# Softmax attention: ScalarE copies turned weights ahead of the next exponential, and TensorE's step goes transposes, value products, scores

## The chip, the cores and the metric

The kernel runs on one core of a Trainium2 chip. The metric is device time in microseconds (us) of one execution; three runs were taken, and their median counts. Five engines of the core matter here: TensorE (PE in the profile; PEld is its loading of stationary operands), ScalarE (ACT), VectorE (DVE), GpSimd (POOL) and the DMA queues, which SyncE (SP) issues.

## The reference, cut to what matters

The program is two transformer blocks of two layers each, on 256 tokens of width 1024 (the second block has 256 context tokens as well), all in float32. Attention with a softmax occurs in three forms, and only these are touched by the change:

```
# first block, both layers: forgetting attention, 8 heads of 64
logits = where(k_pos <= q_pos, q k^T / 8 + decay, -inf)
# second block, both layers: grouped attention and neighbourhood attention, 8 heads of 64
s = q k^T / 8 (+ bias)          # keys: the latent tokens and the context tokens
p = softmax(logits)
y = p v
```

Stick-breaking attention in the first block and the matrix LSTM in the second run through the same functions of the kernel under other mode names ("stick", "mlstm").

## The kernel before, in words

**The stream of products.** Every dense product is made from float32 weights that arrive by DMA in units of 128 x 1024. ScalarE copies a unit to `w_hi` (line 1055, rounded), VectorE makes the remainder `w_lo` (line 1572), and TensorE makes three products, high by high, high by low and low by high (lines 2438 and 2451 in the mode where 128 tokens are the stationary operand). `w_hi` and `w_lo` have three places (`HL`). A unit is done in parts of 128 tokens: with 256 tokens it has two parts, with 512 tokens four. One part is four matmuls of 512 columns with `w_hi` and two with `w_lo`.

**Steps beside the stream.** Attention is cut into steps, and `spread` and `paced_steps` pin each step to a unit and a part of the stream; after that part TensorE runs the step, in program order. ScalarE and VectorE do their share of the steps of unit j - 2 behind their split of unit j (`stream`, `finish_unit`). Each engine has one queue in program order, so a wait in it holds back all that stands behind it. In the dense part of every attention there is one step to a part of the stream, and a new unit begins before an even step. The grouped and the neighbourhood attention have a first stretch too, where the first four steps lie one to a unit.

**Items.** An item is one head with one tile of 128 queries; items come in pairs of two heads. Item k has 128 or 256 keys in the first block, and in the second 512 keys for latent queries and 256 for context queries (layer 0 only). In layer 0 of the second block two pairs of 256 keys and two pairs of 512 keys alternate; in layer 1 all have 512. There are 64 softmax pairs: 8 in each first-block layer, 16 for each of the two attentions in layer 0 of the second block, 8 for each in layer 1.

**What an item goes through.** (1) TensorE: `pair_scores` writes the scores of items k and k + 1 (line 2751; line 2757 adds a bias or a mask where there is one). (2) VectorE: `begin` takes the negated maximum (line 2111). (3) ScalarE: `weights` makes the exponential with its sum (line 1393) into `prob[k % 2]`, once `turn(k - 2)` has read that place. (4) VectorE: `finish` takes the reciprocal and scales the weights (line 2127). (5) TensorE: `turn` transposes them into PSUM bank 6 (line 2768), once the bank has been copied out. (6) ScalarE: `turned_weights` copies the bank to `prob_t` (line 1413). (7) TensorE: `pair_gather` multiplies with the values (line 2788). (8) ScalarE and VectorE: `output` writes the result of a pair in two parts (lines 1425 and 2160).

**Order in one step k, before.** TensorE: at even k `pair_scores(k)`, then `pair_gather(k - 4)`; at every k `turn(k - 2)`. ScalarE: `weights(k)`, `turned_weights(k - 2)`, `output(k - 3)`. VectorE: `begin(k)`, `finish(k - 1)`, `output(k - 3)`. Items are counted so that `output` does something at even k only.

VectorE's part, which the change leaves as it is:

```
if k < n:
    begin(k)
if 1 <= k <= n:
    finish(k - 1)
if k >= 3:
    output(k - 3)
```

Of the kernel before, what the change touches and what calls it, by code (L numbers as in the profile page):

```python
# [212 lines left out]
def build(nc, a, out):  # L213
    ctx = ExitStack()
    with ctx:
# [806 lines left out]
        def _(act):  # L1022
# [359 lines left out]
            def attend(st, k):  # L1382
                k0 = st.at["item"]
                n = len(st.items)

                def weights(i):
                    e, i0 = st.items[i], k0 + i
                    nk = e["nk"]
                    z = ps[:, 4 + i0 % 2, 0:nk]
                    if st.mode == "soft":  # L1390
                        act.wait_ge(max_done, st.at["max"] + i + 1)
                        act.wait_ge(pt_done, i0 - 1)
                        nc.scalar.activation(prob[:, i0 % 2, 0:nk], z, ACT.Exp, bias=att[:, i0 % 2:i0 % 2 + 1],  # L1393
                                             accum_out=att[:, 2 + i0 % 2:3 + i0 % 2]).then_inc(exp_done, 1)
                    elif st.mode == "stick":
                        act.wait_ge(bounded, st.at["bounded"] + i + 1)
                        act.wait_ge(probs_done, i0 - 1)
                        nc.scalar.activation(st.tmp[:, 2 + i0 % 2, 0:nk], st.tmp[:, i0 % 2, 0:nk], ACT.Sigmoid, scale=-1.0)
                        nc.scalar.activation(st.tmp[:, 4 + i0 % 2, 0:nk], st.tmp[:, i0 % 2, 0:nk], ACT.Sigmoid).then_inc(exp_done, 1)
                    else:  # L1400
                        act.wait_ge(scores_done, i0 + 1)
                        act.wait_ge(probs_done, i0 - 1)
                        for d in range(2):
                            ins = nc.scalar.activation(st.decay[:, i0 % 2, d, 0:nk], ps[:, 4 + d, 0:nk], ACT.Exp,
                                                       bias=st.mcols[:, e["t"], 2 + d, e["h"]:e["h"] + 1])
                        ins.then_inc(exp_done, 1)

                def turned_weights(i):
                    e, i0 = st.items[i], k0 + i
                    bank = 7 if st.mode == "mlstm" else 6  # L1410
                    act.wait_ge(pt_done, i0 + 1)
                    act.wait_ge(pv_done, i0 - 1)
                    nc.scalar.activation(prob_t[:, i0 % 2, 0:e["nk"]], ps[:, bank, 0:e["nk"]], ACT.Copy).then_inc(pt_saved, 1)

                def output(i):
                    e, i0 = st.items[i], k0 + i
                    if st.mode == "mlstm":
                        act.wait_ge(pv_done, i0 + 1)
                        nc.scalar.activation(e["dst"], ps[:, 7, 0:P], ACT.Copy).then_inc(ml_saved, 1)
                    elif e["hh"]:  # L1420
                        pr, t = e["y"]
                        act.wait_ge(pv_done, i0 + 1)
                        if i == 1 and st.y_free:
                            act.wait_ge(main.units_used, st.y_free)
                        nc.scalar.activation(st.ys[0][:, pr, t * P:(t + 1) * P], ps[:, 7, 0:P], ACT.Copy).then_inc(y_hi_done, 1)

                if st.mode == "mlstm":
                    i = k // 2
                    if k % 2 == 0 and i >= 3:
                        output(i - 3)  # L1430
                    if k % 2 and i < n:
                        weights(i)
                    if k % 2 and 2 <= i <= n + 1:
                        turned_weights(i - 2)
                    return
                if k < n:
                    weights(k)
                if 2 <= k <= n + 1:
                    turned_weights(k - 2)
                if k >= 3:  # L1440
                    output(k - 3)
# [896 lines left out]
        def _(pe):  # L2338
# [385 lines left out]
            def attend(st, k):  # L2724
                k0 = st.at["item"]
                n = len(st.items)

                def scores(i):
                    e, i0 = st.items[i], k0 + i
                    nk = e["nk"]  # L2730
                    if st.mode == "mlstm":
                        pe.wait_ge(probs_done, i0)
                        pe.wait_ge(exp_done, i0)
                        for d in range(2):
                            dst = ps[:, 4 + d, :]
                            row = row_of_r[:, e["h"], :]
                            mm(dst[:, 0:nk], row, ml_both[:, d, e["k0"]:e["k0"] + nk], start=True, stop=False)
                            mm(dst[:, 0:T], ident_r[:, :], e["masks"][d], start=False, stop=True)
                        mm(ps[:, 6, 0:nk], e["q"], e["k"], start=True, stop=True).then_inc(scores_done, 1)
                        return  # L2740

                def pair_scores(i):

                    pair = [(st.items[i + hh], ps[:, 4 + (k0 + i + hh) % 2, :]) for hh in range(2)]
                    nk = pair[0][0]["nk"]
                    adds = len(pair[0][0]["add"])
                    n_add = T if adds and nk > T else nk
                    pe.wait_ge(exp_done, k0 + i)
                    for lo, hi in ([(0, nk)] if n_add == nk else [(0, n_add), (n_add, nk)]):
                        for e, z in pair:  # L2750
                            ins = mm(z[:, lo:hi], e["q"], e["k"][:, lo:hi], start=lo == 0, stop=not adds)  # L2751
                    for j in range(adds):
                        for e, z in pair:
                            lhs, rhs, ready = e["add"][j]
                            if ready is not None:
                                pe.wait_ge(bias_ready, ready)
                            ins = mm(z[:, 0:n_add], lhs, rhs, start=False, stop=j == adds - 1)  # L2757
                    ins.then_inc(scores_done, 2)

                def turn(i):  # L2760
                    e, i0 = st.items[i], k0 + i
                    bank = 7 if st.mode == "mlstm" else 6
                    pe.wait_ge(probs_done, i0 + 1)
                    pe.wait_ge(pt_saved, i0)
                    if st.mode == "mlstm":
                        pe.wait_ge(ml_saved, st.at["ml"] + i)
                    for c in range(e["nk"] // P):
                        ins = nc.tensor.transpose(ps[:, bank, c * P:(c + 1) * P], prob[:, i0 % 2, c * P:(c + 1) * P],  # L2768
                                                  ident[:, :])
                    ins.then_inc(pt_done, 1)  # L2770

                def gather(i):
                    e, i0 = st.items[i], k0 + i
                    chunks = e["nk"] // P
                    pe.wait_ge(pt_saved, i0 + 1)
                    for c in range(chunks):
                        ins = mm(ps[:, 7, 0:P], prob_t[:, i0 % 2, c * P:(c + 1) * P], e["v"][c],
                                 start=c == 0, stop=c == chunks - 1)
                    ins.then_inc(pv_done, 1)

                def pair_gather(i):

                    chunks = st.items[i]["nk"] // P
                    pe.wait_ge(pt_saved, k0 + i + 2)
                    pe.wait_ge(y_saved, st.at["pair"] + i // 2)
                    for c in range(chunks):
                        for hh in range(2):
                            ins = mm(ps[hh * HD:(hh + 1) * HD, 7, 0:P], st.items[i + hh]["v"][c],  # L2788
                                     prob_t[:, (k0 + i + hh) % 2, c * P:(c + 1) * P], start=c == 0, stop=c == chunks - 1)
                    ins.then_inc(pv_done, 2)  # L2790

                if st.mode == "mlstm":
                    i = k // 2
                    if k % 2 == 0 and i >= 3:
                        gather(i - 3)
                    if k % 2 and i < n:
                        scores(i)
                    if k % 2 and 2 <= i <= n + 1:
                        turn(i - 2)
                    return  # L2800
                if k % 2 == 0 and k < n:
                    pair_scores(k)
                if k % 2 == 0 and k >= 4:
# [104 lines left out]
```

## Time and profile before

| what | value |
|---|---|
| median of 3 runs | 2824.49 us (2823.5 to 2825.09) |
| profiled execution, its own time | 2821.74 us |
| its span in the profile | 2819.9 us |
| granted TensorE clock, mean | 0.983 of full speed |
| TensorE matmul busy | 2671.0 us (95%) |
| VectorE busy | 1677.2 us (59%) |
| ScalarE busy | 1375.5 us (49%) |
| GpSimd busy | 93.4 us (3%) |
| DMA | 444.88 MB, 158 GB/s in the mean |

Times in the profile are counted from the span's start. A row of the timeline gives the start, the duration, the engine and line, what is written from what, the number of instructions merged into the row, and in brackets how long the engine was idle before and what ended the idle time. The softmax attentions lie at about 130 to 190 and 580 to 640 us (forgetting), 1445 to 1555 and 2425 to 2490 us (grouped), 1560 to 1675 and 2494 to 2570 us (neighbourhood).

### The profile page before, as it was taken

What the parts mean: (1) busy time and instruction counts of PE and PEld (TensorE: products, weight loads), DVE (VectorE), ACT (ScalarE), POOL (GpSimd) and SP (SyncE); (2) the same over time, 40 slices, a digit from 0 to 9 for tenths busy, and PEclk for the clock granted to TensorE, in tenths of its full rate; (3) what the DMA queues carried; (4) which work ended last, traced back from release to release, by engine and by line L of the source; (5) the groups of instructions that cost most, each with busy time, mean ns of one, the idle gap of its engine ahead of it and who ended that gap; (6) DMA issues with size and microseconds to landing.
All of it is one profiled execution on the core that took longest, in us unless ns stands there. A gap on an engine that the chain in (4) does not pass through costs nothing.

```text
span 2819.9 us, 40663 instructions
## 1 busy us (share of the span) xinstructions
PE 2671.0 (95%) x14804; PEld 2147.3 (76%) x14804; DVE 1677.2 (59%) x2555; ACT 1375.5 (49%) x2245; POOL 93.4 (3%) x104
## 2 busy tenths in 40 slices
PE   8999999998999999999999999999998899999998
PEld 7668888666888888777776777777777677667997
DVE  5654445646998998354545545553454556455776
ACT  5544345544777776433335344432333544445654
POOL 2000001000000000000000100000000110010000
PEclk9999999999999999899999999999999999999999
DMA  7438895434999997222221213454552234334564
GB/s 227 130 117 263 252 299 161 127 112 165 312 332 323 321 331 264 84 68 60 83 85 50 78 57 105 129 163 134 150 160 73 83 111 114 89 105 119 144 187 142
DMA packets 352459, 444.88 MB, mean 158 GB/s; under 512 B 19616, under 2 KB 197920, under 8 KB 352288
## 3 DMA queue, kind: packets, MB, share of 16 engines
q1 hardware_dynamic: 349792, 435.44, 49.0%
q0 software_dynamic: 2208, 6.79, 0.8%
q8 instruction: 109, 1.79, 0.3%
q14 instruction: 62, 0.51, 0.1%
q10 hardware_dynamic: 288, 0.36, 0.0%
HBM read 441.48 MB, written 1.05 MB: 157 GB/s over the span
## 4 chain that ended last, share of the span: by engine, by line
PE 79%; DVE 8%; ACT 7%; issue 5%; DMA 1%; POOL 0%; ACTq 0%; DVEq 0%; POOLq 0%
PE ps L2410 20%; PE ps L2438 15%; PE ps L2397 14%; PE ps L2451 7%; PE ps L2442 4%; ACT w_hi L1055 2%; PE ps L2647 2%; PE ps L2768 2%; PE ps L2459 2%; PE ps L2751 2%; PE ps L2757 1%; DVE w_lo L1572 1%; PE ps L2788 1%; PE ps L2475 1%; PE ps L2354 1%
## 5 line engine op out<-in xcount | busy, mean ns | idle before, releaser
L1572 DVE TENSOR_TENSOR w_lo<-raw,w_hi 128x1024 fp32r<-128x1024 f32 (+1 forms) x578 | 683.7, 1199 | 511.2 <-ACT w_hi L1055 447.7
L1055 ACT ACTIVATE w_hi<-raw 128x1024 fp32r<-128x1024 f32 (+1 forms) x578 | 585.6, 1030 | 250.1 <-PE ps L2410 120.6
L2438 PE MATMUL ps<-w_hi,h_hi 128*128 128x512 f32 (+1 forms) x992 | 403.7, 409 | 11.5 <-DVE h_lo L2023 4.0
L2438 PE MATMUL ps<-w_hi,h_lo 128*128 128x512 f32 (+1 forms) x992 | 380.2, 385 | 0.0
L2397 PE MATMUL ps<-h_hi,w_hi 128*128 128x256 f32 (+1 forms) x1008 | 300.5, 323 | 16.4 <-ACT w_hi L1055 11.3
L2451 PE MATMUL ps<-w_lo,h_hi 128*128 128x512 f32 (+1 forms) x992 | 298.1, 384 | 0.0
L2397 PE MATMUL ps<-h_lo,w_hi 128*128 128x256 f32 (+1 forms) x1008 | 295.7, 319 | 0.0
L2397 PEld LDWEIGHTS ps<-h_hi,w_hi 128*128 128x128 f32 x1008 | 191.6, 190 | 49.2 <-ACT w_hi L1055 15.3
L2438 PEld LDWEIGHTS ps<-w_hi,h_hi 128*128 128x128 f32 x992 | 188.2, 190 | 48.5 <-issue 12.7
L2451 PEld LDWEIGHTS ps<-w_lo,h_hi 128*128 128x128 f32 x992 | 183.3, 188 | 39.7
L2438 PEld LDWEIGHTS ps<-w_hi,h_lo 128*128 128x128 f32 x992 | 187.9, 189 | 29.0 <-issue 1.0
L2410 PE MATMUL ps<-w_hi,act_hi 128*128 128x512 f32 x528 | 208.2, 394 | 0.0
L1572 DVE TENSOR_TENSOR w_lo<-arena,w_hi 128x1024 fp32r<-128x1024 f32 (+1 forms) x192 | 201.7, 1086 | 7.5 <-ACT w_hi L1055 7.1
L2410 PE MATMUL ps<-w_hi,act_lo 128*128 128x512 f32 x528 | 205.8, 390 | 0.0
L2397 PEld LDWEIGHTS ps<-h_lo,w_hi 128*128 128x128 f32 x1008 | 191.8, 190 | 12.6
L1393 ACT ACTIVATE arena<-ps,att 128x512 f32<-128x512 f32 (+2 forms) x128 | 72.9, 570 | 244.0 <-DVE att L2111 150.6
L1055 ACT ACTIVATE w_hi<-arena 128x1024 fp32r<-128x1024 f32 (+1 forms) x192 | 175.3, 948 | 23.5 <-PE ps L2410 22.8
L2397 PE MATMUL ps<-h_hi,w_lo 128*128 128x256 f32 (+1 forms) x1008 | 177.2, 318 | 0.0
L2397 PEld LDWEIGHTS ps<-h_hi,w_lo 128*128 128x128 f32 x1008 | 149.8, 191 | 13.1
L2410 PE MATMUL ps<-w_lo,act_hi 128*128 128x512 f32 x528 | 149.6, 394 | 0.6
L2410 PE MATMUL ps<-w_hi,h_hi 128*128 128x512 f32 (+1 forms) x384 | 145.7, 379 | 1.6 <-issue 1.4
L2410 PE MATMUL ps<-w_hi,h_lo 128*128 128x512 f32 (+1 forms) x384 | 142.9, 372 | 0.0
(302 smaller groups left out, 4227.5 us busy)
## 6 DMA issues: line engine op xcount, KB each, us to landing
raw<-in_w_in SPq DMA_DIRECT2D x196, 512.0 KB, 3.7
arena<-in_w_mod SPq DMA_DIRECT2D x96, 512.0 KB, 6.0
raw<-in_w_up SPq DMA_DIRECT2D x88, 512.0 KB, 4.4
raw<-in_w_gu_exp SPq DMA_DIRECT2D x64, 512.0 KB, 5.5
arena<-in_w_gu_exp SPq DMA_DIRECT2D x64, 512.0 KB, 5.0
arena<-in_w_gu_exp SPq DMA_DIRECT2D x64, 384.0 KB, 3.9
arena<-in_w_dn_exp SPq DMA_DIRECT2D x48, 512.0 KB, 6.4
raw<-in_w_gu_dense SPq DMA_DIRECT2D x44, 512.0 KB, 8.1
```

Source lines behind the costliest of these rows:

```text
L1055: nc.scalar.activation(w_hi[:, half, 0:n], place[:, 0:n], ACT.Copy).then_inc(seg.sig.hi_ready, 1)
L1393: nc.scalar.activation(prob[:, i0 % 2, 0:nk], z, ACT.Exp, bias=att[:, i0 % 2:i0 % 2 + 1], accum_out=att[:, 2 + i0 % 2:3 + i0 % 2]).then_in ...
L1572: nc.vector.tensor_tensor(w_lo[:, half, 0:n], place[:, 0:n], w_hi[:, half, 0:n].bitcast(F32), ALU.subtract).then_inc(seg.sig.lo_ready, 1)
L2397: ins = mm(dst, w[:, f0:f0 + wide], x[:, k + c, 0:seg.N], start=upper and k + c == 0 and x is ah, stop=not upper and k + c == DC - 1)
L2410: ins = mm(dst, x, w[:, c * width:(c + 1) * width], start=upper and opens and c == 0 and x is xh, stop=not upper and closes and c == m - 1)
L2438: ins = mm(ps[:, 2 * h + p % 2, 0:width], x[:, k + c, p * P:(p + 1) * P], wh[:, c * width:(c + 1) * width], start=opens and c == 0 and x i ...
L2442: ins = mm(ps[0:wide, 2 * h + p % 2, 0:seg.N], wh[:, f0:f0 + wide], x[:, k + c, 0:seg.N], start=opens and c == 0 and x is ah, stop=False)
L2451: ins = mm(ps[:, 2 * h + p % 2, 0:width], ah[:, k + c, p * P:(p + 1) * P], wl[:, c * width:(c + 1) * width], start=False, stop=last and no ...
L2459: ins = mm(ps[0:wide, 2 * h + p % 2, 0:seg.N], wl[:, f0:f0 + wide], ah[:, k + c, 0:seg.N], start=False, stop=last)
L2647: ins = mm(ps[0:wide, bank, cols_], w[:, f0:f0 + wide], x[:, k + c, cols_], start=begins and kind == 0, stop=ends and kind == 2)
L2751: ins = mm(z[:, lo:hi], e["q"], e["k"][:, lo:hi], start=lo == 0, stop=not adds)
L2768: ins = nc.tensor.transpose(ps[:, bank, c * P:(c + 1) * P], prob[:, i0 % 2, c * P:(c + 1) * P], ident[:, :])
```

## The change

In mode "soft" alone, ScalarE's step becomes `turned_weights(k - 2)`, `weights(k)`, `output(k - 3)`, and TensorE's even step becomes `turn(k - 2)`, `pair_gather(k - 4)`, `pair_scores(k)`; an odd step is `turn(k - 2)` as before. VectorE's order stays. No instruction is added or removed, and no wait is written differently; the modes "stick" and "mlstm" keep their order.

```
@@ attend, ScalarE
+                if st.mode == "soft" and 2 <= k <= n + 1:
+                    turned_weights(k - 2)
                 if k < n:
                     weights(k)
-                if 2 <= k <= n + 1:
+                if st.mode != "soft" and 2 <= k <= n + 1:
                     turned_weights(k - 2)
                 if k >= 3:
                     output(k - 3)
@@ attend, TensorE
+                if st.mode == "soft":
+                    if 2 <= k <= n + 1:
+                        turn(k - 2)
+                    if k % 2 == 0 and k >= 4:
+                        pair_gather(k - 4)
+                    if k % 2 == 0 and k < n:
+                        pair_scores(k)
+                    return
                 if k % 2 == 0 and k < n:
                     pair_scores(k)
                 if k % 2 == 0 and k >= 4:
                     pair_gather(k - 4)
```

## Rows read from the trace of the kernel before

**Rows 1.** The page: busy time, share of the span and instructions of each engine.
```profile
PE 2671.0 (95%) x14804; PEld 2147.3 (76%) x14804; DVE 1677.2 (59%) x2555; ACT 1375.5 (49%) x2245; POOL 93.4 (3%) x104
```

**Rows 2.** Line 2768, the transposes of all modes: its idle time, us and times.
```profile
  issue: 31.9, 123
  DVE arena L2127: 15.7, 27
```

**Rows 3.** Timeline of PEld, layer 1, grouped attention: one pair of steps.
```profile
2450.81 0.30 PEld L2751 LDWEIGHTS ps<-arena 64*128 64x128 f32 x4 [0.35 <-ACT arena L1393]
2451.87 0.85 PEld L2788 LDWEIGHTS ps<-arena 128*64 128x64 f32 x16 [0.76 <-ACT arena L1413]
2452.89 0.42 PEld L2768 LDWEIGHTS ps<-ident,arena 128*128 128x128 f32 x4 [0.17 <-issue]
...
2455.33 0.42 PEld L2768 LDWEIGHTS ps<-ident,arena 128*128 128x128 f32 x4 [0.82 <-DVE arena L2127]
...
2457.30 0.30 PEld L2751 LDWEIGHTS ps<-arena 64*128 64x128 f32 x4 [0.36 <-ACT arena L1393]
```

**Rows 4.** Timeline of ACT over the same pair of steps.
```profile
2453.95 0.69 ACT L1393 ACTIVATE arena<-ps,att 128x512 f32<-128x512 f32 x1 [1.89 <-DVE att L2111]
...
2454.63 0.59 ACT L1413 ACTIVATE arena<-ps 128x512 f32<-128x512 f32 x1
2455.11 0.28 ACT L1425 ACTIVATE y_hi<-ps 128x128 fp32r<-128x128 f32 x1
...
2457.50 1.05 ACT L1055 ACTIVATE w_hi<-raw 128x1024 fp32r<-128x1024 f32 x1
```

**Rows 5.** Timeline of DVE over the same pair of steps.
```profile
2452.09 1.23 DVE L1572 TENSOR_TENSOR w_lo<-raw,w_hi 128x1024 fp32r<-128x1024 f32 x1 [1.69 <-ACT w_hi L1055]
2453.23 0.68 DVE L2111 TENSOR_REDUCE att<-ps 128x1 f32<-128x512 f32 x1
...
2455.42 0.29 DVE L2160 TENSOR_TENSOR y_lo<-ps,y_hi 128x128 fp32r<-128x128 f32 x1 [0.91 <-ACT y_hi L1425]
2455.62 0.68 DVE L2111 TENSOR_REDUCE att<-ps 128x1 f32<-128x512 f32 x1
...
2456.41 0.49 DVE L2127 TENSOR_SCALAR arena<-arena,att 128x512 f32<-128x512 f32 x1
```

**Rows 6.** Timeline, layer 0, grouped: scores of 512 keys and an unhindered maximum.
```profile
1475.79 0.30 PEld L2751 LDWEIGHTS ps<-arena 64*128 64x128 f32 x4 [0.44 <-ACT arena L1393]
...
1476.97 0.69 DVE L2111 TENSOR_REDUCE att<-ps 128x1 f32<-128x512 f32 x1 [1.45 <-PE ps L2751]
```

**Rows 7.** Timelines, layer 1, neighbourhood: scores with bias, and their maximum.
```profile
2494.55 0.73 PEld L2751 LDWEIGHTS ps<-arena 64*128 64x128 f32 x8 [0.35 <-issue]
...
2496.79 0.69 DVE L2111 TENSOR_REDUCE att<-ps 128x1 f32<-128x512 f32 x1 [3.35 <-PE ps L2757]
```

**Rows 8.** Timeline of PEld, layer 0, grouped: a step after scores of 256 keys.
```profile
1510.55 0.85 PEld L2788 LDWEIGHTS ps<-arena 128*64 128x64 f32 x16 [0.33 <-issue]
...
1513.06 0.33 PEld L2768 LDWEIGHTS ps<-ident,arena 128*128 128x128 f32 x2
...
1514.97 0.30 PEld L2751 LDWEIGHTS ps<-arena 64*128 64x128 f32 x4 [0.39 <-ACT arena L1393]
```

**Rows 9.** Timeline of PEld: scores of steps 4 and 28, layer 0, grouped.
```profile
1469.72 0.30 PEld L2751 LDWEIGHTS ps<-arena 64*128 64x128 f32 x4 [1.37 <-ACT arena L1393]
...
1537.85 0.30 PEld L2751 LDWEIGHTS ps<-arena 64*128 64x128 f32 x4 [0.36 <-issue]
```

**Rows 10.** The same, layer 0, neighbourhood.
```profile
1584.65 0.73 PEld L2751 LDWEIGHTS ps<-arena 64*128 64x128 f32 x8 [2.32 <-ACT arena L1393]
...
1657.08 0.73 PEld L2751 LDWEIGHTS ps<-arena 64*128 64x128 f32 x8 [0.37 <-issue]
```

**Rows 11.** The same, layer 1, neighbourhood: scores of steps 8 and 14.
```profile
2531.47 0.73 PEld L2751 LDWEIGHTS ps<-arena 64*128 64x128 f32 x8 [0.36 <-ACT arena L1393]
...
2553.25 0.73 PEld L2751 LDWEIGHTS ps<-arena 64*128 64x128 f32 x8 [0.36 <-ACT arena L1393]
```

## The prediction

> **What bounds the kernel now.** I read the page first: TensorE is busy for 95% of the span, VectorE for 59%, ScalarE for 49% [rows 1]. So the program ends earlier only if TensorE's queue is held less in the attention steps, or gets through them in less time. Then the line view of the transposes: in front of line 2768 the loading of operands sat idle for 31.9 us under "issue" and 15.7 us behind VectorE [rows 2], the largest idle time among the softmax attention's TensorE lines. It covers all modes and also holds a gap of 0.17 us in front of each even step's transposes, which is there without any wait.
>
> Then the timeline, one pair of steps in the grouped attention of layer 1 [rows 3]. Step 6 starts at 2450.81 with the scores, 1.06 later come the value products (a gap of 0.76, as the scores still stream), 1.02 later the transposes. The odd step's transposes start at 2455.33, 2.44 after the even ones, with 0.82 us idle before them. Where nothing is waited for, a stretch of the stream behind transposes takes about 1.2: from the odd transposes to the next scores it is 1.97, less 0.42 for the transposes and 0.36 for the gap before the scores. So 2.44 holds 0.8 of waiting. What it waits for: `turn(7 - 2)` needs bank 6, so `turned_weights(6 - 2)`, the copy at 2454.63, behind the exponential at 2453.95 [rows 4], which waited for the maximum at 2453.23, which stood behind a `w_lo` of 1.23 us at 2452.09 [rows 5]. The copy itself could have started two microseconds earlier: it sits behind an exponential with which it has nothing to do.
>
> **The change part by part.** Nothing is added or removed; two orders change. All times below are for items of 512 keys. T is the start of the even step, s the start of its scores.
>
> *ScalarE's copy first.* The copy of item k - 2 then needs only the transposes at T and the value products that follow, so it runs at about T + 1.7, long before the odd transposes. The 0.8 of waiting goes. But exponential k can no longer be held by transposes either; it waits for its maximum alone.
>
> *TensorE's order.* Before, transposes k had from s to the end of the next step's scores and products. Now they are the first thing in step k + 2. The ring that must close in one pair is: scores, maximum k, exponential k, first output part, second output part, maximum k + 1 (VectorE's order is unchanged), scaling k, transposes k. From rows: scores to maximum 1.18 where nothing hinders it [rows 6]; to the exponential 0.72 (maximum at 2453.23, exponential at 2453.95); to the next ScalarE instruction 0.68 [rows 4], which is now the output and no longer the copy (0.48 saved); to VectorE's output 0.31; to maximum k + 1 0.20; to the scaling 0.79; scaling 0.49 [rows 5]; a hop to TensorE of 0.05, as between the other links. Sum 4.42. TensorE's own work from s to the next T is scores 1.06, stream 1.25, transposes 0.42, stream 1.2, or 3.93. So the ring ends last and a new wait of 0.5 arises at T. It is queued in front of value products and scores, and so all the stream waits for it.
>
> From T to s: transposes 0.42, a gap, products 0.85, a gap. What is the gap between transposes and products, and between products and scores? The trace has neither. Behind products, whose matmuls have 128 columns, the gap is 0.17; behind the stream's 512 columns it is 0.36; behind scores 0.33 [rows 8] to 0.76 [rows 3]. In both new places the work in front is 128 columns wide, so I take 0.17 twice; the ends are 0 and 0.36. With 0.17: s = T + 1.61, and the pair takes 4.42 + 1.61 = 6.03 against 6.49 now. The Trainium skill, TensorEngine Tiling (Array Packing), Key Properties, says that changing the tiling mode drains TensorE. Counted by that rule alone, an unbiased pair has three changes of mode before and after, and a biased one four before and three after, so the order itself would save nothing in the first; the rows add that the length of a gap goes with what is being drained.
>
> *VectorE's and ScalarE's splits.* These stand in the queues before an even step. `w_hi` starts at exponential k + 1 plus 1.16 now (2457.50, against a maximum k + 1 at 2455.62 and 0.72 more) [rows 4, 5]; without the copy it is 0.68, so at s + 3.1 (maximum k + 1) + 0.72 + 0.68 = s + 4.5, ending at s + 5.55. `w_lo` follows until s + 6.8, and maximum k + 2 is due at s + 6.03 + 1.18 = s + 7.2. The split that now delays every such maximum by more than a microsecond fits with 0.4 to spare.
>
> *256 keys.* Scores take 0.63 (the products start 0.33 behind 0.30 of loading [rows 8]). The ring is shorter by about 1.2 (each pass over half the columns), near 3.2; TensorE's work from s to the next T is 0.63 + 1.25 + 0.42 or 0.2 + 1.2 = 3.3 to 3.5. No wait.
>
> **The sum.** Layer 1, grouped: six intervals of 6.49 - 6.03, 2.8 us. Layer 0, grouped: now 68.13 from step 4 to step 28, which is three rounds of four pairs, 22.7 each [rows 9]. After: ring 4.42 twice, 3.5 and 3.4 for the short pairs, and from T to s 1.0, 1.2, 1.6, 1.4 (short and long products and transposes), 20.9; three rounds 5.3 us, with the half round behind them some 5.7. Neighbourhood: with the bias the maximum starts 2.24 behind the scores [rows 7], so its ring is 5.48 and the pair 7.09, against 21.78 / 3 = 7.26 in layer 1 [rows 11]: six intervals, 1.0 us. In layer 0, 72.43 / 3 = 24.14 per round [rows 10] against 20.9 + 2 x 1.06 = 23.1: 3.2 us for three rounds and the rest. Forgetting attention has 128 and 256 keys, and masks that lengthen TensorE's part, so no ring; I give each of 16 pairs the narrower gap in front of its scores, 0.36 - 0.17, 3 us in both layers together. The long waits at the start of the attentions, 1.37 and 2.32 before step 4's scores [rows 9, 10], come from a maximum behind the branches' evacuation; then the transposes wait for a scaling of the same moment, so they stay. Together 2.8 + 5.7 + 1.0 + 3.2 + 3 = 15.7 us. The profiled execution took 2821.74 (span 2819.9), 2.75 below the median; the difference applies to the median of 2824.49 alike: 2808.8, say 2809.
>
> **The rivals.**
>
> *A, forecast:* the waits at the odd transposes go, the ring takes part of it back: 10 to 25 us less, 2799 to 2814. Chance 0.64.
>
> *B, the ring doesn't bind:* if some link is shorter than the rows say, only the removal counts. All idle time of rows 2 is 47.6; less 0.17 in 64 even steps (10.9), less the other modes' and some tenths that the matmuls cover, about 21 remains, and with narrower gaps (64 x 0.19 = 12) the gain is 33: 2791. Against it: each link is a row. Chance 0.08.
>
> *C, the gain is eaten by gaps:* if the two new gaps are 0.36 each as behind the stream, every pair is 0.38 longer, 24 us over 64 pairs; 15.7 - 24 gives 2833, and with half of that 2821, near no change. For it: the trace has neither sequence. Against it: 0.17 behind 128 columns. Of this 0.12 for a result within 6 us of no change, 0.04 above.
>
> *D, slower, a split falls into the ring:* if `w_lo` reaches VectorE less than 1.2 before maximum k is due, the maximum is late by up to 1.23, and the ring passes it on to the stream in full. It decides from 0.4 us of lateness of `w_hi` on. In layer 1 every pair has a split (12 pairs), in layer 0 one pair in two (14): 26 x 1.23 = 32 us lost, minus 15.7, gives 2841; at half the lateness 2825. For it: the slack of 0.4 is small, and ScalarE's tanh of a finished gate stands in the same queue. Against it: the order of VectorE's queue, where `w_lo` comes only after scaling k. Chance 0.12, half of it slower by more than 0.2%.
>
> **How the numbers follow.** About 0.2%, 5.6 us, is what a measurement of this kernel can tell from no change. Faster by more: A, B, 0.03 of C's milder forms, 0.75. Within: 0.09 + 0.05 = 0.14. Slower: 0.04 + 0.07 = 0.11. The range leaves out B's far end and the ends of C and D: 2797 to 2825; A alone 2799 to 2814.
>
> **What the profile after would show.** The copy of line 1413 in front of the exponential, no idle time before odd transposes; new idle time of about 0.5, put down to VectorE's line 2127, in front of even transposes of 512-key pairs; 6.03 from even step to even step in layer 1's grouped attention; gaps of 0.17 in front of products and scores. A gap of 0.36 there speaks for C; a `w_lo` directly before a late maximum k for D; no wait at even transposes for B. I would be wrong in the sign if exponential or maximum stood behind something else that is now late, above all transposes k - 1, whose copy now precedes exponential k + 1 by only some hundredths.

## The result, and the profile after

The changed kernel takes 2815.91 us in the median of 18 runs (2809.76 to 2820.32), beside 2825.41 us in 18 runs of the kernel before (2822.54 to 2827.85): a ratio of 0.9968, 95% interval 0.9961 to 0.9975, 9.5 us less. The forecast was 15.7 us less, 2809, in a range of 2797 to 2825; the measured time lies in that range and some 2 us above rival A's own, 2799 to 2814. The profiled execution took 2815.94 us (span 2814.2).

| stretch, first scores to last value products | before | after | forecast gain | gain |
|---|---|---|---|---|
| forgetting, both layers | 58.29 + 59.51 | 59.29 + 58.20 | 3.0 | 0.3 |
| layer 0, grouped | 106.51 | 103.27 | 5.7 | 3.2 |
| layer 0, neighbourhood | 113.54 | 112.22 | 3.2 | 1.3 |
| layer 1, grouped | 63.47 | 60.30 | 2.8 | 3.2 |
| layer 1, neighbourhood | 72.50 | 72.46 | 1.0 | 0.0 |

Times are us, from the timelines of TensorE's loading, one profile of each kernel. The gains add up to 8.1 us. The two profiled spans differ by 5.7 us, since the parts of the program outside these stretches took 2.4 us more in the profile after. How layer 1's gain is split between its two rows is not firm: in the repeated run of the changed kernel (`h1_change_again`) they read 58.80 and 74.00, with the same sum.

The page of the changed kernel, busy time of each engine (answers to [rows 1]): TensorE does the same work.

```profile
PE 2672.0 (95%) x14804; PEld 2149.9 (76%) x14804; DVE 1676.5 (60%) x2555; ACT 1383.7 (49%) x2245; POOL 95.1 (3%) x104
```

The line of the transposes, now line 2770, idle time before it (answers to [rows 2]), first of the changed kernel, then the third line of the same view of the kernel before, which [rows 2] leaves out:

```profile
  DVE arena L2129: 57.1, 86
  issue: 12.0, 50
```

```profile
  ACT arena L1413: 6.4, 15
```

So the idle time in front of the transposes grew from 54.0 to 69.1 us while the kernel got faster. Over the three lines of the attention (transposes, scores and value products in all modes, without the waits for lines that only other modes have) it shrank: in front of the scores the wait for the exponential (40.6 us before) is gone, in front of the value products 34.3 us became 14.7. This view adds the idle time of the loading and that of the matmuls. Taken apart, the loading's fell from 119.3 to 84.9 us, by 34, and the matmuls' own from 23.5 to 17.2, by 6.3; the time fell by 9.5. Idle time of the loading is mostly not idle time of the matmuls.

The pair of steps in layer 1's grouped attention, loading on TensorE in the changed kernel (answers to [rows 3]; 2770 transposes, 2790 products, 2753 scores):

```profile
2453.59 0.42 PEld L2770 LDWEIGHTS ps<-ident,arena 128*128 128x128 f32 x4 [0.29 <-DVE arena L2129]
2454.18 0.85 PEld L2790 LDWEIGHTS ps<-arena 128*64 128x64 f32 x16 [0.17 <-issue]
2455.20 0.30 PEld L2753 LDWEIGHTS ps<-arena 64*128 64x128 f32 x4 [0.17 <-issue]
...
2457.72 0.42 PEld L2770 LDWEIGHTS ps<-ident,arena 128*128 128x128 f32 x4 [0.21 <-DVE arena L2129]
...
2459.62 0.42 PEld L2770 LDWEIGHTS ps<-ident,arena 128*128 128x128 f32 x4 [0.28 <-DVE arena L2129]
```

From even step to even step 6.03 us, as forecast, and the scores start 1.61 behind the even transposes, as forecast. But the matmuls leave no room in it. The same loop in windows (span of time, its length, busy time of each engine), first of the kernel before, then of the changed one:

```profile
2450.81:2457.30 6.49, 6.08 (x41) 4.04 (x40) 3.83 (x8) 3.64 (x9) 0.00 (x0) 1.00 0.29 81
```

```profile
2453.59:2459.62 6.03, 6.03 (x42) 4.07 (x41) 3.92 (x8) 3.86 (x10) 0.00 (x0) 1.00 0.29 90
```

Before, TensorE's matmuls stood still for 0.41 us of each pair; now for none. The row of the matmuls in the kernel before shows where, in front of the odd transposes, and names the copy:

```profile
2455.36 0.63 PE L2768 MATMUL ps<-ident,arena 128*128 128x128 f32 x4 [0.41 <-ACT arena L1413]
```

The loading's row of the same transposes has 0.82 and names VectorE [rows 3]; half of that time the matmuls in flight had covered.

ScalarE and VectorE in the changed kernel (answers to [rows 4, 5]):

```profile
2455.38 0.60 ACT L1413 ACTIVATE arena<-ps 128x512 f32<-128x512 f32 x1 [0.68 <-PE ps L2790]
2457.11 0.69 ACT L1393 ACTIVATE arena<-ps,att 128x512 f32<-128x512 f32 x1 [1.13 <-DVE att L2113]
...
2457.78 0.27 ACT L1425 ACTIVATE y_hi<-ps 128x128 fp32r<-128x128 f32 x1
```

```profile
2454.74 1.23 DVE L1574 TENSOR_TENSOR w_lo<-raw,w_hi 128x1024 fp32r<-128x1024 f32 x1 [1.20 <-ACT w_hi L1055]
2456.38 0.69 DVE L2113 TENSOR_REDUCE att<-ps 128x1 f32<-128x512 f32 x1 [0.42 <-PE ps L2753]
...
2458.08 0.29 DVE L2162 TENSOR_TENSOR y_lo<-ps,y_hi 128x128 fp32r<-128x128 f32 x1 [0.42 <-ACT y_hi L1425]
2458.29 0.68 DVE L2113 TENSOR_REDUCE att<-ps 128x1 f32<-128x512 f32 x1
...
2459.08 0.49 DVE L2129 TENSOR_SCALAR arena<-arena,att 128x512 f32<-128x512 f32 x1
```

The copy stands ahead of the exponential and waits for nobody's maximum. `w_lo` ends 0.42 us before the even maximum can start, so rival D's split is out of the way. The odd maximum follows `y_lo` directly: the ring of the prediction (a closed chain of waits, in which each pair of steps waits for the one before), link by link. From the scores at 2455.20 to the transposes at 2459.62 it takes 4.42.

### The profile page after: what moved, and what is told of

Same layout as the page of the kernel before. It is cut to its first block, busy times and chain, and to the rows that moved or that the text cites. A ratio compares the mean times of both kernels' runs of the same rounds, so it can differ in the third digit from the quotient of the medians.

```text
span 2814.2 us, 40663 instructions
## 1 busy us (share of the span) xinstructions
PE 2672.0 (95%) x14804; PEld 2149.9 (76%) x14804; DVE 1676.5 (60%) x2555; ACT 1383.7 (49%) x2245; POOL 95.1 (3%) x104
## 4 chain that ended last, share of the span: by engine, by line
PE 82%; DVE 8%; ACT 5%; issue 4%; POOL 0%; DVEq 0%; ACTq 0%; POOLq 0%
PE ps L2412 20%; PE ps L2440 17%; PE ps L2399 14%; PE ps L2453 8%; PE ps L2444 4%; PE ps L2753 2%; PE ps L2770 2%; ACT w_hi L1055 2%; PE ps L2649 2%; PE ps L2461 2%; PE ps L2790 2%; PE ps L2759 1%; PE ps L2477 1%; DVE w_lo L1574 1%; PE ps L2356 1%
```

## The experiments

All ratios are against runs of the kernel before on the same chip. "Pair" is the loop in layer 1's grouped attention, 6.49 before and 6.03 after the change.

### Each half of the change alone

`e1_scalar_only`: the edit on ScalarE is made, the one on TensorE isn't. `e2_tensor_only`: the reverse.

> ScalarE's order of the change with TensorE's order of before. Theory (a wait for the copy goes, and what then ends last is a chain through both outputs and the second maximum): the idle time before the odd transposes goes, but the exponential now waits for transposes and for the copy, and the exponential of item k + 1 reaches the next scores late: about 6.05 us from even step to even step in layer 1's grouped attention, nearly the 6.03 of the full change, so about 2816 us in all. Rival (TensorE's order is what gains): no better than before, 2825. Rival (the copy's wait is all there is, and TensorE's new order costs something): about 5.75 from even step to even step and 2805.

> TensorE's order of the change with ScalarE's order of before. Theory: the copy is back between exponential and output, so the ring from scores to transposes is 0.48 longer, 4.90 and with 1.61 up to the scores 6.51 in layer 1's grouped attention (before: 6.49), 7.57 in its neighbourhood attention (before: 7.26); in all 2824 to 2830. Rival (TensorE's order gains by itself, through narrower gaps): 2815 or less.

ScalarE's order alone: 2816.01 us, ratio 0.9964 (0.9952 to 0.9977), as expected and as much as the whole change; the pair takes 6.00, with matmuls in 5.96 of it. TensorE's order alone: 2861.89 us, ratio 1.0131 (1.0116 to 1.0146); the pair takes 7.28, far over what was expected. ScalarE's rows in that kernel, and TensorE's loading of two sets of transposes, show why:

```profile
2491.38 0.59 ACT L1413 ACTIVATE arena<-ps 128x512 f32<-128x512 f32 x1
2491.85 0.28 ACT L1425 ACTIVATE y_hi<-ps 128x128 fp32r<-128x128 f32 x1
2493.09 0.69 ACT L1393 ACTIVATE arena<-ps,att 128x512 f32<-128x512 f32 x1 [0.96 <-DVE att L2111]
...
2493.77 0.58 ACT L1413 ACTIVATE arena<-ps 128x512 f32<-128x512 f32 x1
```

```profile
2492.08 0.42 PEld L2768 LDWEIGHTS ps<-ident,arena 128*128 128x128 f32 x4 [1.00 <-DVE arena L2127]
2494.47 0.42 PEld L2768 LDWEIGHTS ps<-ident,arena 128*128 128x128 f32 x4 [0.78 <-DVE arena L2127]
```

Each set of transposes starts 0.70 behind a copy (2491.38, 2493.77), because that copy frees their bank. The row of the loading names VectorE's scaling, which had ended 0.8 before; the row of the matmuls names the copy:

```profile
2494.50 0.63 PE L2768 MATMUL ps<-ident,arena 128*128 128x128 f32 x4 [0.37 <-ACT arena L1413]
```

The ring from the scores (2488.80) runs over the maximum 1.17, exponential 0.73, copy 0.68, y_hi 0.47, y_lo 0.31, maximum 0.21, exponential 0.72, copy 0.68 and transposes 0.70, 5.67 in all, and 1.61 more lead to the next scores: 7.28. The expectation had missed that the transposes wait for the copy and not only for the scaling.

### VectorE's scaling in front of the maximum

`e3_scale_first` is the changed kernel, `g2_before_scale_first` the kernel before, both with

```
+                if st.mode == "soft" and 1 <= k <= n:
+                    finish(k - 1)
                 if k < n:
                     begin(k)
-                if 1 <= k <= n:
+                if st.mode != "soft" and 1 <= k <= n:
                     finish(k - 1)
```

> The changed kernel with one more order: VectorE's step of a softmax attention is scaling k - 1, maximum k, output. This takes maximum k + 1 (0.79 us) out of the ring that ends in transposes k. Theory (the ring sets the pair): idle time before the transposes of 512-key pairs goes, 5.75 instead of 6.03 from even step to even step in layer 1's grouped attention, 6.5 to 6.8 instead of 7.08 in its neighbourhood attention, some 10 us less than the changed kernel: about 2806. Rival (TensorE's own work sets the pair, and the waits seen only fill its shadow): no difference from the changed kernel, 2816.

It took 2818.26 us, ratio 0.9974 (0.9964 to 0.9985), nothing gained where 2806 was expected. Its VectorE rows:

```profile
2456.32 0.68 DVE L2113 TENSOR_REDUCE att<-ps 128x1 f32<-128x512 f32 x1
2458.79 1.23 DVE L1574 TENSOR_TENSOR w_lo<-raw,w_hi 128x1024 fp32r<-128x1024 f32 x1 [1.79 <-ACT w_hi L1055]
...
2460.12 0.49 DVE L2129 TENSOR_SCALAR arena<-arena,att 128x512 f32<-128x512 f32 x1
2460.53 0.68 DVE L2113 TENSOR_REDUCE att<-ps 128x1 f32<-128x512 f32 x1
2462.22 0.29 DVE L2162 TENSOR_TENSOR y_lo<-ps,y_hi 128x128 fp32r<-128x128 f32 x1 [1.01 <-ACT y_hi L1425]
...
2463.02 0.68 DVE L2113 TENSOR_REDUCE att<-ps 128x1 f32<-128x512 f32 x1
```

From odd maximum to odd maximum it takes 6.70 us (2456.32 to 2463.02), with no link on TensorE: maximum, exponential, `w_hi`, `w_lo`, scaling, even maximum, exponential, `y_hi`, `y_lo`, scaling, odd maximum. The split of the stream is a part of it. So there is a ring of ScalarE and VectorE that the prediction had not looked for. It did not set every pair of this kernel: the even transposes around it lie 6.09 to 7.25 apart. Layer 1's grouped attention took 64.50 us instead of 60.30, its neighbourhood attention 70.82 instead of 72.46. In the kernel before, the same walk through its rows gives: exponential 0.72, copy 0.68, `w_hi` 0.48, `w_lo` 1.08, maximum 1.14, exponential 0.72, copy 0.68, `y_hi` 0.48, `y_lo` 0.31, maximum 0.20, together 6.49, its pair to the hundredth [rows 3 to 5]. That gave a number to test:

> The kernel before, with VectorE's scaling of item k - 1 put in front of maximum k. Theory 1 (a ring of ScalarE and VectorE sets the pair in the kernel before): both scalings come into that ring: maximum k + 1, exponential 0.72, copy 0.68, w_hi 0.48, w_lo 1.08, reciprocal 1.14, scaling 0.19, maximum 0.41, exponential 0.72, copy 0.68, y_hi 0.48, y_lo 0.31, reciprocal 0.20, scaling 0.19, maximum 0.40: the pair in layer 1's grouped attention goes from 6.49 to 7.68, and the kernel to 2845 or more. Rival (the transposes' wait is what costs, and it ends with a scaling): scaling earlier shortens it, the pair goes below 6.49, and the kernel below 2825.

Measured: 2863.93 us, ratio 1.0135 (1.0120 to 1.0151), and the pair (scores to scores):

```profile
2483.59 0.30 PEld L2753 LDWEIGHTS ps<-arena 64*128 64x128 f32 x4 [0.72 <-ACT arena L1393]
...
2491.27 0.30 PEld L2753 LDWEIGHTS ps<-arena 64*128 64x128 f32 x4 [0.82 <-ACT arena L1393]
```

The pair took 7.68, the sum of the links, and 32 pairs of 512 keys by 1.19 more are 38 us of the 40 that the kernel lost. In the kernel before, then, ScalarE and VectorE set the pace of the 512-key pairs, and the wait at the odd transposes was not what set it.

### Scores as the second part of the step

`e4_scores_second` has ScalarE's old order, and TensorE's even step as transposes, scores, value products.

```
                     if 2 <= k <= n + 1:
                         turn(k - 2)
+                    if k % 2 == 0 and k < n:
+                        pair_scores(k)
                     if k % 2 == 0 and k >= 4:
                         pair_gather(k - 4)
-                    if k % 2 == 0 and k < n:
-                        pair_scores(k)
```

> TensorE's even step goes transposes, scores, value products, with ScalarE's order of before. The scores start 1.02 us earlier in the step, so the ring has 1.02 more room, and the copy of line 1413, which is back in it, costs 0.48. Theory: the ring closes before TensorE is through, about 5.75 in layer 1's grouped attention and 2806 in all. Rival (the scores' place doesn't matter, only the copy's): as before or as with TensorE's order alone, 2825.

2837.20 us, ratio 1.0043 (1.0030 to 1.0056), slower than before, where the theory had 2806 and the rival 2825. The steady pair again takes 6.49 (even transposes at 2455.31, 2461.80 and 2468.29), which fits: TensorE's order isn't in that ring. By stretches most of the loss lies in layer 0, 109.15 and 118.67 us against 106.51 and 113.54; the forgetting attentions and layer 1's neighbourhood attention lost 1.8 each. At the starts of the attentions the transposes wait up to 3.84 us for a scaling. It was not taken apart further.

### Opening the ring of the changed kernel

VectorE's `output` of a pair (`y_lo`) moves from the even step into the next odd one, behind the scaling, so the odd maximum no longer stands behind it:

```
-                if k >= 3:
+                if st.mode == "soft":
+                    if k % 2 and 5 <= k <= n + 1:
+                        output(k - 4)
+                    if k == n + 2:
+                        output(n - 1)
+                elif k >= 3:
                     output(k - 3)
```

> The changed kernel, with VectorE's second output part (y_lo) moved one step later, behind scaling k, so that maximum k + 1 no longer stands behind y_lo. That opens the ring which sets the even transposes' wait: scores to transposes would be about 3.7 and no longer 4.42. Theory 1 (TensorE is full: the matmul rows of the changed kernel cover 6.03 of a pair's 6.03 us, and a pair in the scale-first kernel that waited for nothing took 5.95): the pair in layer 1's grouped attention goes from 6.03 to 5.95, and the kernel gains 1 to 3 us, to about 2814. Rival (the prediction's own count, 3.93 of TensorE's work behind the scores and 1.61 in front of them): the pair goes to 5.55, and the kernel gains 0.48 in some 28 pairs, to about 2803.

> The kernel before, with only that move in VectorE's queue. Theory 1: the 6.49 us of a pair are a ring of ScalarE and VectorE alone (maximum k + 1, exponential 0.72, copy 0.68, w_hi 0.48, w_lo 1.08, maximum 1.14, exponential 0.72, copy 0.68, y_hi 0.48, y_lo 0.31, maximum k + 1 0.20: sum 6.49), and the wait at the odd transposes is only what TensorE shows of it. The move takes y_hi, y_lo out of the ring: pair about 6.0, TensorE's own work, and the kernel near 2816, as much as the whole change, with its two edits left out. Rival (the prediction's reading: the copy behind the exponential in front of the odd transposes costs 0.8): that copy stays, so the pair stays at 6.4 to 6.5 and the kernel at 2825.

> ScalarE's new order alone, with that move in VectorE's queue. Theory 1: with ScalarE's order alone a pair takes 6.00, with a wait of 0.48 in front of the scores, but matmuls fill 5.96 of it; the move opens that ring, the wait goes, the pair stays at 5.95 to 6.00, and the kernel stays at 2814 to 2816. Rival (idle time in front of the scores is lost time): pair about 5.8, some 28 times 0.12 to 0.2 us less, about 2811.

On the changed kernel: 2810.54 us, ratio 0.9950 (0.9937 to 0.9964). The pair is 5.95, not 5.55 (transposes 2446.49 to 2452.44), and matmuls fill it:

```profile
2446.49 0.59 PEld L2775 LDWEIGHTS ps<-ident,arena 128*128 128x128 f32 x4
2447.24 0.85 PEld L2795 LDWEIGHTS ps<-arena 128*64 128x64 f32 x16 [0.17 <-issue]
...
2450.78 0.42 PEld L2775 LDWEIGHTS ps<-ident,arena 128*128 128x128 f32 x4 [0.21 <-DVE arena L2129]
2452.44 0.59 PEld L2775 LDWEIGHTS ps<-ident,arena 128*128 128x128 f32 x4
```

```profile
2446.49:2452.44 5.95, 5.95 (x42) 4.14 (x41) 3.83 (x8) 3.75 (x9) 0.00 (x0) 1.00 0.30 91
```

Now that the even transposes wait for nothing, their loading takes 0.59 instead of 0.42 and starts without a gap. A wait of a few tenths in this place, as in the changed kernel, costs the matmuls little: there the pair takes only 0.08 more. The kernel takes some 5 us less than the changed one, where a gain of 1 to 3 was expected. By stretches that is 1.7 and 0.4 us in layer 0 (grouped, neighbourhood) and 1.9 and 1.0 in layer 1; the 0.08 of a steady pair explain only a part, and the rest was not taken apart.

With ScalarE's order alone, the same move gives 2812.99 us, ratio 0.9958 (0.9945 to 0.9972), pair 5.91; 5.95 to 6.00 and 2814 to 2816 us were expected, and the rival had 5.8 and 2811. The time lies between the two, so the rows have to decide. The idle time of 0.39 in front of its scores stays in the rows and costs nothing: matmuls fill 5.91 of 5.91. Beside the same move on the changed kernel (0.9950) this is within the intervals, so again TensorE's order shows no gain that can be told.

On the kernel before it gives 2821.32 us, ratio 0.9987 (0.9978 to 0.9996), pair 6.24. The direction is theory 1's, the size isn't. Its ScalarE rows show a link that the expectation lacked:

```profile
2460.62 0.59 ACT L1413 ACTIVATE arena<-ps 128x512 f32<-128x512 f32 x1
...
2462.08 0.69 ACT L1393 ACTIVATE arena<-ps,att 128x512 f32<-128x512 f32 x1 [0.70 <-PE ps L2773]
```

The odd exponential waits for transposes k - 1, which free its place in `prob`; they wait for the copy at 2460.62. With `y_lo` gone, this path of 1.46 takes the place of the one over `y_hi`, `y_lo` and the maximum (0.48 + 0.31 + 0.20 + 0.72 = 1.71), and 6.49 less 0.25 is 6.24. So both 6.0 and the rival's "no change" are refuted. The path that now binds runs through the wait that the prediction had read in [rows 3, 4], copy before odd transposes; in the kernel before it was 0.25 shorter than the one that set the pace.

### Lengthening the ring

```
+                        if i % 2:
+                            settled(nc.vector.tensor_reduce(att[:, i0 % 2:i0 % 2 + 1], z, AX.X, ALU.max, negate=True))
                         nc.vector.tensor_reduce(att[:, i0 % 2:i0 % 2 + 1], z, AX.X, ALU.max, negate=True).then_inc(max_done, 1)
```

> The changed kernel, in which VectorE takes the maximum of every odd item twice (one more reduction of about 0.60 us and a short wait for its own end). Theory 1 (the ring scores, maximum k, exponential, y_hi, y_lo, maximum k + 1, scaling k, transposes k binds in pairs of 512 keys): the pair in layer 1's grouped attention goes from 6.03 to 6.65 to 6.75, and the kernel loses 0.6 to 0.7 us in some 28 pairs, to about 2833. Rival (the idle time in front of the even transposes is covered by matmuls already in TensorE's queue, and the ring does not bind): the pair grows by 0.2 at most, and the kernel stays under 2820.

2850.15 us, ratio 1.0087 (1.0074 to 1.0101). The second maximum starts 0.72 behind the first (0.68 and a short wait), and the pair becomes 6.75, 0.72 longer:

```profile
2480.03 0.68 DVE L2114 TENSOR_REDUCE att<-ps 128x1 f32<-128x512 f32 x1
2480.75 0.69 DVE L2115 TENSOR_REDUCE att<-ps 128x1 f32<-128x512 f32 x1
```

```profile
2482.09 0.42 PEld L2772 LDWEIGHTS ps<-ident,arena 128*128 128x128 f32 x4 [1.01 <-DVE arena L2131]
...
2488.84 0.42 PEld L2772 LDWEIGHTS ps<-ident,arena 128*128 128x128 f32 x4 [1.01 <-DVE arena L2131]
```

The ring binds, so rival B is refuted in the 512-key pairs. The total rose by 34 us over the changed kernel, not by 17. The two grouped attentions lost 6.0 us each, which is eight pairs of 512 keys by 0.72, 5.8; the neighbourhood attentions, with as many such pairs, lost 10.3 and 7.2, the forgetting ones 1.8. So the expectation had counted too few pairs (32, not 28, and 0.72 each). That leaves 4.5 us in layer 0's neighbourhood attention and 1.4 in layer 1's. Rows of layer 0 show most of the 4.5:

```profile
1605.16 1.48 DVE L2131 TENSOR_SCALAR arena<-arena,att 128x512 f32<-128x512 f32 x1
```

```profile
1606.69 0.42 PEld L2772 LDWEIGHTS ps<-ident,arena 128*128 128x128 f32 x4 [2.00 <-DVE arena L2131]
```

Four scalings there ran beside an addition on GpSimd and took 1.28 to 1.56 us instead of 0.49, 3.9 us more together; in the changed kernel none did in that attention. The last round without such a scaling (even transposes of steps 20 to 28) took 24.99 against 23.48 in the changed kernel, 1.51 more, where its two doubled maxima are worth 1.44. The 1.4 of layer 1 stay unexplained. All stretches together lost 31.4 us, as much as the two profiled spans differ (31.8).

### The forgetting attentions

`g1_forgetting_old` is the changed kernel, in which both edits apply only where `max(e["nk"] for e in st.items) > 256`; the forgetting attentions keep the old orders.

> The changed kernel, in which the forgetting attentions of the first block keep both old orders. The prediction gave these 16 pairs 3 us, a gap of 0.17 in place of 0.36 in front of each pair's scores. If that term is right, this kernel is 3 us slower than the changed one, near 2819. Theory 1: a gap in the loading of operands behind matmuls that still stream is no time of TensorE's, so a shorter one saves nothing; the stretches of the two forgetting attentions together are 117.5 us in the changed kernel and 117.8 in the one before, and this kernel stays at 2816.

2816.54 us, ratio 0.9973 (0.9962 to 0.9984), beside 0.9968 for the whole change: the forgetting attentions contribute nothing that can be measured, where the prediction had given them 3 us.

### Once more, side by side

> The changed kernel once more, to be compared with the next one on the same chip: 2816, ratio 0.9968, a pair of 6.03 in layer 1's grouped attention.

> The changed kernel with y_lo one step later, once more beside the changed kernel. If the gain that the two ratios suggest is real (0.995 against 0.9968), it takes 3 to 7 us less than the changed kernel in the same call: near 2811, a pair of 5.95. If it was the spread between calls, both are within 2 us of each other.

The changed kernel: 2815.11 us (2812.49 to 2817.08), ratio 0.9962 (0.9949 to 0.9976). With `y_lo` later: 2810.47 us (2808.56 to 2811.86), ratio 0.9946 (0.9933 to 0.9960). The runs of the two don't overlap: 4.6 us less than the change, 14.9 less than the kernel before.

## Why the prediction was right, and where its size was off

**Faster, by removing a wait: right.** ScalarE's order does it, and alone it gives all of the gain. TensorE's new order contributes nothing that can be told beside it (0.9964 without it, 0.9968 with it) and costs 37 us without it. The prediction had treated both as one gain.

**What the wait was: half right.** The copy behind the exponential was late, as argued. The prediction counted it at 0.8 us a pair from the loading's row; the matmuls stood still for 0.41. And the chain that set the pace before went on from the copy, over the splits and back to VectorE, and closed at 6.49 without TensorE. Moving the copies takes two links of 0.48 out of that ring: the others add up to 5.53, less than a pair on TensorE. The prediction also called the idle time in front of the transposes the largest of these lines; in front of the scores it was 40.6 us behind the exponential and 14.0 under "issue".

**The ring of 4.42 and the pair of 6.03: right** in every link, and shown to bind by the doubled maximum. The pair in layer 1's neighbourhood attention was forecast at 7.09; even steps lie 7.08 apart there where nothing disturbs them.

**The step that failed is the price of TensorE's own work**, "TensorE's own work from s to the next T" of 3.93, with 1.61 in front 5.54 in a pair. With `y_lo` moved, the pair takes 5.95, and matmuls fill it. In its rows the value products start 0.75 behind the even transposes, where the prediction has 0.42 and 0.17; the stream behind the scores takes 1.46, where it has 1.25; and from odd to even transposes it is 1.66, where it has 1.62. The 0.4 us were hidden in the idle gaps of the loading, which the prediction counted as time to be had: behind a wait the transposes load in 0.42; in a full queue they load in 0.59, beside matmuls that still run. In layer 1 the ring was longer anyway, so this changed nothing. In layer 0 it did. There the prediction took 20.9 for a round of four pairs, in which the short pairs go by TensorE's own work. Even transposes of steps 4, 12, 20 and 28 in the changed kernel:

```profile
1470.06 0.20 PEld L2770 LDWEIGHTS ps<-ident,arena 128*128 128x128 f32 x2 [1.24 <-DVE arena L2129]
...
1491.50 0.38 PEld L2770 LDWEIGHTS ps<-ident,arena 128*128 128x128 f32 x2
...
1513.37 0.20 PEld L2770 LDWEIGHTS ps<-ident,arena 128*128 128x128 f32 x2 [0.27 <-issue]
...
1535.06 0.38 PEld L2770 LDWEIGHTS ps<-ident,arena 128*128 128x128 f32 x2
```

21.44, 21.87 and 21.69 us, 65.0 in all, where 62.7 was forecast and 68.13 stood before [rows 9]. In the neighbourhood attention the even transposes of steps 4 and 28 lie 70.94 apart, where 69.3 was forecast. With the ring opened (`f1_after_output_later`), a round still takes 21.2 (scores at 1474.50 and 1495.66), and matmuls fill all of it: that is TensorE's floor in this order.

**The narrower gaps: 3 us forecast, nothing measured.** The gap in front of the scores did become 0.17, as forecast, and it bought nothing, by the stretches (0.3) and by the experiment. The Trainium skill, Perfetto Trace Analysis, section Tensor Engine Instruction (MATMUL, LD_WEIGHTS), says that loads can be pulled ahead of matmuls in flight, and that the end of a TensorE instruction in a profile is estimated. The rows here agree with the first: loading stands idle while the matmuls' window is full.

**Layer 1's neighbourhood attention: 1.0 us forecast, none came.** Its start takes as long as before, as the prediction said (29.68 us from the first scores to the first instruction of step 6, now its transposes; 29.66 before, to its scores), and three of the four pairs of steps from 6 to 14 take 7.08. The other took 8.04 (scores at 2527.22 and 2535.26), so 0.96 of the 1.0 us went there. Rows of VectorE, GpSimd and TensorE's loading in it:

```profile
2530.25 1.53 DVE L2129 TENSOR_SCALAR arena<-arena,att 128x512 f32<-128x512 f32 x1
```

```profile
2530.22 1.27 POOL L1018 TENSOR_TENSOR arena<-arena,window 128x512 f32<-128x512 f32 x1 [2.43 <-DMA arena<-in_position_bias]
```

```profile
2531.83 0.42 PEld L2770 LDWEIGHTS ps<-ident,arena 128*128 128x128 f32 x4 [1.46 <-DVE arena L2129]
```

A scaling of 0.49 took 1.53, about as long as GpSimd's addition beside it ran, and the transposes waited 1.46 for it. The same happened in the repeated run of the change, whose pair took 8.06. Scalings were stretched before as well (1.39 at 1596.84), but there one could be late without TensorE waiting; in the ring of 4.42, here 5.48 with the bias, it can't.

Of the rivals, C is refuted in its place (both new gaps are 0.17), although its idea, that gaps aren't what they seem, came true in another form; D did not happen (0.42 of slack, 0.4 forecast); B is refuted by the doubled maximum.

## What to carry to other kernels

Before pricing a reordering, walk the queues of the helper engines for a ring that closes without the bottleneck engine; its links, taken from start to start, add up to the loop time to the hundredth if it is the one that binds, and a planned edit can be priced on it, if the next longest path is walked too: the two scalings put into the ring of the kernel before were priced to the hundredth (7.68), while the move of `y_lo` in the kernel before was priced at 6.0 and took 6.24. Take the bottleneck's own floor from the busy time of its matmuls in a window, never from the idle gaps of its loading: those went down by 34 us for 9.5 us of time, the matmuls' own by 6.3. After the fix, look for the next instruction that stands in the new ring without belonging to it; here moving one such VectorE instruction gave another 4.6 us.

## What the hardware showed unexpectedly

VectorE's scaling of 128 x 512, when it starts while GpSimd's `tensor_tensor` (1.27 us) runs, lasts until that has ended and 0.3 longer: 1.53 and, in the repeated run, 1.54 us at the same place, where 0.49 is usual. The 14 kept traces have 22 such scalings (two of them started 0.03 and 0.04 before the addition), 0.62 to 1.59 us long, and each ends 0.28 to 0.30 behind the GpSimd instruction; 31 others that started 0.11 or more before it kept their 0.48 or 0.49. `w_lo` took 1.45 instead of 1.23. The Trainium skill, SBUF — State Buffer, section SBUF: two separate sides, says that VectorE, in some of its instructions, and GpSimd share a pair of ports, which one instruction holds for its whole length; these rows agree.

What a row names as the end of an idle time was wrong by a whole engine where two waits stood in front of one group: the loading's row named VectorE's scaling for the transposes, when it was ScalarE's copy that came 0.70 before each of them. The row of the same transposes' matmuls named the copy.
